# Order in which the matmuls of w_up and w_down walk the columns of their moving operand and of PSUM

## The reference, cut to what matters

```python
h = rmsnorm(x, norm_mix_g)
proj = einsum('btd,de->bte', h, w_in)            # 2048 -> 3072
...                                              # conv, RG-LRU, causal pooling
x = x + einsum('bte,ed->btd', y_mix, w_out)      # 2048 -> 2048
h2 = rmsnorm(x, norm_mlp_g)
f = relu(einsum('btd,df->btf', h2, w_up))        # 2048 -> 8192
x = x + einsum('btf,fd->btd', f * f, w_down)     # 8192 -> 2048
y = rmsnorm(x, norm_final_g)
```

## Time and profile before

| | |
|---|---|
| median of 3 runs | 1843.9 us (1842.42 to 1844.52) |
| span of the profiled execution | 1841.4 us |
| TensorE busy | 1812.1 us (98%), 15,016 matmuls and as many weight loads |
| VectorE, ScalarE, GpSimd busy | 1478.1 us (80%), 924.6 us (50%), 132.9 us (7%) |
| mean granted clock of TensorE | 0.998 |
| DMA | 288 MB, 157 GB/s |

### The profile page before, as it was taken

The page is one execution under the profiler, slowest core; times in us unless marked ns, Lnnn a source line. Parts: engine busy times, 40 slices in busy tenths (PEclk is TensorE's granted clock), DMA queues, the critical chain, the costliest instruction groups (busy, mean ns, idle before and its releaser), DMA issues. The chain is left out here.

```text
span 1841.4 us, 38079 instructions
## 1 busy us (share of the span) xinstructions
PE 1812.1 (98%) x15016; PEld 1805.0 (98%) x15016; DVE 1478.1 (80%) x2039; ACT 924.6 (50%) x1322; POOL 132.9 (7%) x224
## 2 busy tenths in 40 slices
PE   7999999999999999999999999899999999999998
PEld 7999999999999999999999999899999999999998
DVE  7777785545488888888888888899888888889897
ACT  6555533333344454454445445555555555556565
POOL 3000000200000000000000000110000000001100
PEclk9999999999999999999999999999999999999999
DMA  8333333344354444544444452788666776767742
GB/s 275 103 92 91 97 98 93 116 152 139 99 171 148 160 146 163 173 135 156 148 161 146 143 173 90 213 233 238 185 179 179 199 181 181 192 168 206 230 114 93
DMA packets 209979, 288.19 MB, mean 157 GB/s; under 512 B 9437, under 2 KB 186089, under 8 KB 209808
## 3 DMA queue, kind: packets, MB, share of 16 engines
q1 hardware_dynamic: 185552, 186.75, 33.0%
q0 software_dynamic: 23984, 99.19, 18.7%
q10 hardware_dynamic: 288, 0.11, 0.0%
HBM read 222.00 MB, written 64.53 MB: 156 GB/s over the span
## 5 line engine op out<-in xcount | busy, mean ns | idle before, releaser
L897 PE MATMUL ps<-forms,u_high 128*128 128x260 f32 x2688 | 490.4, 282 | 0.7 <-DVE product_parts L1833 0.7
L897 PEld LDWEIGHTS ps<-forms,u_high 128*128 128x128 f32 x2688 | 413.0, 188 | 0.9 <-issue 0.9
L897 PE MATMUL ps<-forms,u_low 128*128 128x260 f32 x1344 | 374.8, 282 | 0.6 <-DVE u_low L1823 0.6
L897 PE MATMUL ps<-forms,d_high 128*128 128x260 f32 x2240 | 373.6, 283 | 1.0 <-DVE product_parts L1833 1.0
L897 PEld LDWEIGHTS ps<-forms,d_high 128*128 128x128 f32 x2240 | 314.4, 188 | 1.2 <-ACT d_high L1180 1.1
L897 PE MATMUL ps<-f_forms,d_high 128*128 128x260 f32 x1344 | 265.4, 283 | 4.2 <-ACT d_high L1180 1.6
L897 PEld LDWEIGHTS ps<-forms,u_low 128*128 128x128 f32 x1344 | 250.7, 188 | 0.8 <-DVE u_low L1823 0.8
L1363 DVE TENSOR_TENSOR w_low<-raw,w_high 128x512 fp32r<-128x512 f32 x160 | 109.0, 689 | 137.0 <-ACT w_high L992 135.8
L897 PEld LDWEIGHTS ps<-f_forms,d_high 128*128 128x128 f32 x1344 | 204.9, 188 | 6.7 <-ACT d_high L1180 3.7
L897 PE MATMUL ps<-forms,d_low 128*128 128x260 f32 x1120 | 192.5, 283 | 0.0
L992 ACT ACTIVATE w_high<-raw 128x512 fp32r<-128x512 f32 x160 | 99.4, 628 | 180.7 <-PE ps L704 174.6
(11 more groups left out here) (305 smaller groups left out, 3578.5 us busy)
## 6 DMA issues: line engine op xcount, KB each, us to landing
even_rows<-in_w_up_dram SPq DMA_DIRECT2D x32, 1024.0 KB, 5.6
odd_rows<-in_w_up_dram SPq DMA_DIRECT2D x32, 1024.0 KB, 5.8
d_even<-in_w_down_dram SPq DMA_DIRECT2D x33, 768.0 KB, 7.1
d_odd<-in_w_down_dram SPq DMA_DIRECT2D x33, 768.0 KB, 5.2
raw<-in_w_in_dram SPq DMA_DIRECT2D x96, 256.0 KB, 2.7
sums_spill<-part_out POOLq DMA_DIRECT2D x40, 520.0 KB, 5.4
scratch<-f_spill POOLq DMA_DIRECT2D x20, 910.0 KB, 7.1
f_spill<-f_out POOLq DMA_DIRECT2D x32, 520.0 KB, 4.7
```

The lines of the kernel that those rows point to most:

```text
L897: mm = pe.matmul(out, w[:, k, :], x[:, form, :], start=(PRODUCT_OPENS[r] and at == 0), stop=at == len(steps) - 1, skip_group_check=True)
```

## The change

The product's matmuls read the same 260 columns and write the same 260 places in PSUM, but in another order. The columns are cut into 65 groups of four. The old order is groups 0, 1, 2, ... 64. The new one is 0, 13, 26, 39, 52, then 1, 14, 27, 40, 53, and so on in 13 sweeps. Input and output have the same order, so every sum lands at its old place, and who reads PSUM reads as before.

The 38 fillers are replaced by 42: seven each of six patterns in which they read the first set in groups of four, five of them of 256 columns (sweeps over every 8th, 16th, 32nd, 2nd group; every 4th group with the sweeps in reverse order) and one of 260 (every 6th group in one sweep). All of them write PSUM without gaps.

```diff
+LINE_STEP = 13
...
-WARM = 14 * (512,) + 24 * (128,)
...
+            def by_lines(half):
+
+                return half.rearrange("p (m n e) -> p n m e", n=LINE_STEP, e=4)
+
             def product(m, r):
...
-                out = ps[:, bank_at, 0:HALF]
+                out = by_lines(ps[:, bank_at, 0:HALF])
...
-                    mm = pe.matmul(out, w[:, k, :], x[:, form, :], start=(PRODUCT_OPENS[r] and at == 0), stop=at == len(steps) - 1,
+                    mm = pe.matmul(out, w[:, k, :], by_lines(x[:, form, :]), start=(PRODUCT_OPENS[r] and at == 0), stop=at == len(steps) - 1,
...
-            for n in WARM:
-                x = s_high[0][:, S3:S3 + (2 if n > HALF else 1), 0:min(n, PROMPT // 2)]
-                pe.matmul(ps[:, BANK_D, 0:n], s_high[0][:, A11, 0:P], x, start=True, stop=True)
+            first_set = s_high[0].rearrange("p r t -> p (r t)")
+            for times, w, x in (
+                (7, first_set[:, 0:P], first_set[:, 256:512].rearrange("p (l s e) -> p s l e", s=8, e=4)),
+                (7, first_set[:, 0:P], first_set[:, 256:512].rearrange("p (l s e) -> p s l e", s=16, e=4)),
+                (7, first_set[:, 0:P], first_set[:, 256:512].rearrange("p (l s e) -> p s l e", s=32, e=4)),
+                (7, first_set[:, 0:P], first_set[:, 256:512].rearrange("p (l s e) -> p s l e", s=2, e=4)),
+                (7, first_set[:, 0:P], first_set[:, 256:1816].rearrange("p (l s e) -> p l s e", s=6, e=4)[:, :, 0, :]),
+                (7, first_set[:, 0:P], first_set[:, 256:512].rearrange("p (l s e) -> p s l e", s=4, e=4)[:, ::-1]),
+            ):
...
+                for _ in range(times):
+                    pe.matmul(into, w, x, start=True, stop=True)
```

More of the change, by code:

```diff
@@ L902, in _ @@
             pe.wait_ge(s_hi, 2)
-            for n in WARM:
-                x = s_high[0][:, S3:S3 + (2 if n > HALF else 1), 0:min(n, PROMPT // 2)]
-                pe.matmul(ps[:, BANK_D, 0:n], s_high[0][:, A11, 0:P], x, start=True, stop=True)
+            first_set = s_high[0].rearrange("p r t -> p (r t)")
[7 more added lines that the diff above has]
+            ):
+                into = ps[:, BANK_D, 0:x.shape[1] * (x.shape[2] if len(x.shape) > 2 else 1) * (x.shape[3] if len(x.shape) > 3 else 1)]
+                if len(x.shape) == 3:
+                    into = into.rearrange("p (a b) -> p a b", b=x.shape[-1])
+                if len(x.shape) == 4:
+                    into = into.rearrange("p (a b c) -> p a b c", b=x.shape[-2], c=x.shape[-1])
+                for _ in range(times):
+                    pe.matmul(into, w, x, start=True, stop=True)
             for m in range(UP_PAIRS):
```

## The result

The changed kernel takes 2025.61 us (median of 3 runs, 2024.18 to 2027.18) where the kernel before takes 1843.9: 1.099 times as long, 95% interval 1.097 to 1.101. Forecast were 1822 and a range of 1765 to 1925.

The account below looks back on a forecast made before the run. The prediction took the MLP's 10,752 matmuls times their pace on TensorE as the bound; 1841.4 - 21.5 for reads, 0 for PSUM writes and fillers, gave 1819.9 us of span, plus 2.5 to the median: 1822, range 1765 to 1925 us.

Parts of the forecast that it names:

- What bounds the kernel: MLP on TensorE: its time is 10,752 matmuls times their pace; one nanosecond is 10.75 us, 0.58% of the kernel.
- What the pace is made of: Product's matmuls, about 120 ns: 108.3 ns of columns, about 1.7 ns fixed, some 10 ns lost while columns stream.
- What that loss depends on: w_up's turns repeat after three weight slots, so SBUF addresses of TensorE's column and weight reads set the some 10 ns.
- Reads in 13 sweeps: Product's matmuls: jumps in the columns' stream avoid part of the loss, 2.0 ns a matmul, 21.5 us off.
- The lower bound of 110 ns: Product's matmuls: at best all of the loss goes, down to the transposes' 110.0 ns, 10.0 ns or 107.5 us off.
- The chosen fifth: Product's matmuls: the share of the streaming loss taken as avoided by the sweeps, 2.0 ns a matmul.
- PSUM written in the same sweeps: Product's PSUM writes: groups of four stay together, each place is written once a matmul; nothing taken.
- Fillers: Fillers before the product's third matmul: they end earlier or later and nothing follows; taken as 0.
- The one on the other side: Product's column reads: jumps back cost or the walk clashes more with weights; 1848 to 1902 us; 22%.
- the second rival: Product's matmuls: a price for each group or PSUM line; one clock per group 291 us, half-rate writes 1,011 us; 13%.
- What would show it: Signs: w_up turns 19.8 us apart; fillers differing by pattern mean SBUF, product alone growing means PSUM; w_in, w_out keep pace.
- equal turns: Starts of w_up's turns: if they become equal at 18.5 us, the loss is gone.

Follow-up runs that it names:

- the scan of the step: Kernel before with further groups of 28 fillers, steps 1 to 27 groups, 128 columns, weights of 32 columns: plain 59 ns, step 5 68, 6 82, 7 63, 16 73.
- step 5: Changed kernel with reads and writes in 5 sweeps over every 5th group in place of 13 over every 13th: 2010.49 us, ratio 1.091.

## Why the prediction was wrong

**What bounds the kernel** was right: the time of the MLP is 10,752 times the pace, one nanosecond is 10.75 us, and the change acted on the pace. 17.9 ns more a matmul are 192 us. From the first product's start to the start of the transposes behind the last one (516.49 to 1824.58 before, 513.49 to 2005.46 after) it is 184. The other 8 us are waits that shrank: of the starts in the product, 33 came 200 ns or more after the one before, and 16 in the changed kernel, and what these hold beyond the pace fell from 13.8 to 5.6 us. The MLP also started 3 us earlier.

**What the pace is made of** had one wrong reading beside a right one. The loss while columns stream is there. But the 110 ns of the transposes are not 260 columns and 1.7 ns fixed: 128 columns took 109.6 ns beside weights of 128 (L933) and 59 beside weights of 32, in the scan of the step. It is the size of the weight load that shows in them, and that it equals the bare time of 260 columns is chance.

**What that loss depends on** is the step that failed. From turns that repeat by the three weight slots the prediction took that the loss hangs on the addresses of both streams, columns and weights, and then that a walk in jumps breaks up clashes between them. The repetition only shows that the weights' place changes the loss a little (118.6 to 121.4 ns here). It doesn't show that the loss comes from the weights. With a quarter of the weight load plain reads are 0.5 ns faster, not 8. The runs showed in its place that the price of the sweeps is the columns' stream's own and is set by its step: 18 ns more with 13 forwards, by reads alone as by both, and 2 ns less with 13 backwards. No row of the trace before could give that step's price, because nearly all that its matmuls read at full pace had step 1.

**Reads in 13 sweeps**, -2.0 ns: the term was of the wrong sign, +18 ns. The lower bound of 110 ns was never near; the cheapest walks found take 116 ns for 256 columns. The chosen fifth was close to what a step of 3 gives (1.5 to 2.2 ns), by luck: it needs the opposite direction.

**PSUM written in the same sweeps**, 0: right (ratio 1.0002). **Fillers**, 0: right; the third matmul waited for `u_low` after (1.03 us at 514.95) as before.

**The rivals.** The one on the other side, that the new walk clashes more, had 22% and a price for each sweep, up to 58 us; the next had one clock for each of 65 groups, 291 us. The truth, 182 us, lay between them in a gap that neither bound covered. The first had the right sign and also named a walk that clashes more with the weights, which the short weights rule out, and a price for each sweep, which step 5 rules out. Two estimates match two of the sizes: 0.83 ns (a clock at 1.2 GHz) for every second group is 65 / 2 x 0.83 = 27 ns over the bare 110 of 260 columns, where 137 to 138 were measured; and for each group, with every 6th, 54 ns, where 162 to 164 were. They say nothing of the steps in between, and no run tests them; what in the memory sets the prices is open. The range should have reached to the second rival, since nothing in the rows bounded a stepped read from above.

**What would show it** named the right signs: fillers differed between the six patterns, so it was SBUF's side; w_in kept its pace. One case was missing: equal turns were foreseen only at 18.5 us, with the loss gone, and they came at 23.15, with a loss that is larger and regular.

## What to carry to other kernels

Where TensorE reads float32 columns at full rate, the step between one 16-byte group and the next, counted modulo 256 bytes, sets the pace: avoid walks that go in steps of 5, 6, 13 or 16 throughout (8 and 10 cost 8 to 9 ns too), mind the sign, and try 3, for which a walk of 13 sweeps backwards gave 1%. A lone step of 5 at the end of each sweep cost nothing here, so a walk of mixed steps is to be measured and not added up. And let the groups begin at whole groups: shifted by 8 bytes, every stepped read took 225 to 231 ns. Before a loss is put down to two streams, take one of them away: matmuls whose result nobody reads, on lines of their own, 28 of a kind, gave a whole table of prices in one run. And where the operation in question has no row at all in the trace, bound it by a run or keep the range open on that side.

## What was not expected of the hardware

- Direction matters: 1851.69 us backwards and 2010.49 us forwards over the same 5 sweeps; every 6th group 162 ns forwards and 127 backwards, every 10th the other way round.
- PSUM took stepped writes in groups of four float32 at no cost (0.9992 to 1.0011).
- Two columns of every four, in one line of 16 bytes, took 6.40 us / 28 = 228 ns for 256 columns (L993, and the same for one of every two). The Trainium skill, "SBUF — State Buffer", section Specifications, has two or more hits on a line as what full bandwidth needs; if two were enough here, these would take some 118 ns, an estimate from the plain reads. For columns at full rate in this format two were not enough and four were; three were not tried.
- The granted clock fell to 0.50 (window 540 to 560 us of the run with fewer rows) with TensorE issuing matmuls back to back; before it fell they had gone from 128 to 64 of its rows, at 528 us. Whether the rows are the cause was not tried.
